# Removing the dummy matmuls that TensorE runs while it waits

## What is computed

```python
def _layernorm(x, g, b):
    mu = xf.mean(-1, keepdims=True)
    var = jnp.square(xf - mu).mean(-1, keepdims=True)
    return (xf - mu) * lax.rsqrt(var + LN_EPS) * g + b
...
    h_lat = _layernorm(ALPHA * h_lat + gt_m * mix, p['ln1_g'], p['ln1_b'])  # "ln1"
    moe = _hier_moe(_modulate(h_lat, sh_f, sc_f), p)  # routing 0, 32 experts
    h_lat = _layernorm(ALPHA * h_lat + gt_f * moe, p['ln2_g'], p['ln2_b'])  # "ln2"
...
        hn = rms_norm(h, attn_norm_g[l])  # "attn"
        proj = hn @ w_in[l]
...
        h = h + merged @ w_out[l]
        hn = rms_norm(h, ffn_norm_g[l])  # "ffn"
        h = h + hierarchical_moe(hn, ...)  # routing 1, 16 experts
    return rms_norm(h, final_norm_g)  # "final"
```

## Time and profile before

| | |
|---|---|
| median of 3 runs | 1681.69 us (1679.67 to 1684.29) |
| span of the profiled execution | 1681.9 us |
| TensorE busy | 1625.6 us, 97% of the span |
| DVE, ACT busy | 513.2 us, 295.8 us |
| granted TensorE clock, mean | 0.987 |

### The profile page before, as it was taken

The page is one execution under the profiler, slowest core; times in us unless marked ns, Lnnn a source line. Parts: engine busy times, 40 slices in busy tenths (PEclk is TensorE's granted clock), DMA queues, the critical chain, the costliest instruction groups (busy, mean ns, idle before and its releaser), DMA issues.

```text
span 1681.9 us, 22604 instructions
## 1 busy us (share of the span) xinstructions
PE 1625.6 (97%) x9324; PEld 1045.2 (62%) x9324; DVE 513.2 (31%) x1141; ACT 295.8 (18%) x470; POOL 16.7 (1%) x37
## 2 busy tenths in 40 slices
PE   5999999999999999999999999999999899999997
PEld 2877644664788885555555555557788775555554
DVE  1447685552001234222222222224023241222223
ACT  1100100221111012222122212222112022222222
POOL 0000000000000000000000000000100000000000
PEclk7999999999999999999999999999999999999999
DMA  9423231564333245999999999993632138999994
GB/s 393 178 100 113 100 113 56 214 243 161 131 126 144 101 164 196 396 416 414 406 412 414 408 413 403 411 388 127 187 143 100 51 150 338 413 403 417 409 410 180
DMA packets 33426, 434.88 MB, mean 259 GB/s; under 512 B 4048, under 2 KB 5592, under 8 KB 7144
## 3 DMA queue, kind: packets, MB, share of 16 engines
q1 hardware_dynamic: 29376, 423.64, 62.7%
q10 hardware_dynamic: 2328, 6.11, 1.5%
q0 software_dynamic: 1680, 4.52, 0.8%
HBM read 431.63 MB, written 2.62 MB: 258 GB/s over the span
## 4 chain that ended last, share of the span: by engine, by line
PE 91%; DVE 4%; DMA 1%; ACT 1%; issue 0%; ACTq 0%; DVEq 0%; SPq 0%
PE PP L629 24%; PE PP L878 20%; PE PP L635 12%; PE PP L905 10%; PE MB L855 6%; PE PP L841 5%; PE PP L847 2%; DMA ring<-in_w_moe 1%; PE MB L777 1%; PE PP L619 1%; PE PP L898 1%; PE MB L720 1%; PE MB L702 1%; PE MB L723 1%; PE MB L768 1%; PE PP L651 1%
## 5 line engine op out<-in xcount | busy, mean ns | idle before, releaser
L878 PE MATMUL PP<-ring,qd 128*64 128x256 f32 x3200 | 362.7, 379 | 2.2 <-ACT qd L541 1.8
L878 PEld LDWEIGHTS PP<-ring,qd 128*64 128x64 f32 x3200 | 228.8, 137 | 162.3 <-issue 35.0
L629 PE MATMUL PP<-uT,ring 128*128 128x256 f32 x1152 | 255.3, 384 | 3.7 <-ACT uT L389 2.7
L629 PEld LDWEIGHTS PP<-uT,ring 128*128 128x128 f32 x1152 | 221.7, 193 | 36.6 <-ACT uT L389 2.8
L905 PE MATMUL PP<-ring,qd 128*64 128x512 f32 x800 | 182.7, 599 | 0.0
L635 PE MATMUL PP<-ring,uT 128*128 128x512 f32 x288 | 125.0, 593 | 0.0
L1070 DVE SCALAR_TENSOR_TENSOR conv<-zpad,vec,conv 128x256 f32<-128x256 f32 x240 | 116.4, 485 | 8.6
L855 PE MATMUL MB<-V 64*128 64x256 f32 x832 | 117.5, 402 | 1.6 <-DVE V L1377 1.6
L905 PEld LDWEIGHTS PP<-ring,qd 128*64 128x64 f32 x800 | 52.9, 137 | 102.3 <-issue 102.3
L841 PE MATMUL PP<-Kc,V 128*64 128x512 f32 x416 | 98.2, 593 | 0.8 <-DVE V L1336 0.8
L635 PEld LDWEIGHTS PP<-ring,uT 128*128 128x128 f32 x288 | 54.5, 190 | 67.0 <-issue 66.9
(11 more groups left out here) (271 smaller groups left out, 1242.7 us busy)
## 6 DMA issues: line engine op xcount, KB each, us to landing
ring<-in_w_moe SPq DMA_DIRECT2D x150, 2048.0 KB, 10.6
ring<-in_w_ada SPq DMA_DIRECT2D x12, 2048.0 KB, 8.2
ring<-in_w_gates SPq DMA_DIRECT2D x8, 2048.0 KB, 7.8
ring<-in_w_v SPq DMA_DIRECT2D x5, 2048.0 KB, 7.7
ring<-in_w_glu SPq DMA_DIRECT2D x4, 2048.0 KB, 16.3
ring<-in_w_g SPq DMA_DIRECT2D x4, 2048.0 KB, 7.8
ring<-in_w_ret SPq DMA_DIRECT2D x4, 2048.0 KB, 7.6
ring<-in_w_q SPq DMA_DIRECT2D x3, 2048.0 KB, 9.6
```

The costliest lines, as they stand in the source:

```text
L629: ins = pe.matmul(out[:, c, :], W[:, k * width + at:k * width + at + P], X[:, k, :], start=k == 0, stop=k == K - 1)
L878: ins = pe.matmul(bank[q][SLOTS * g:SLOTS * (g + 1), 0:L], xts[:, k % 4, SLOTS * (k // 4):SLOTS * (k // 4 + 1)], ring[:, q, k * 512 + g * ...
```

## The change

All calls of keep_clock go, with the function, its constants and its table of PSUM regions. Nothing else changes: no wait, no order, no operand.

```diff
-MEAN_WAIT, SQUARE_WAIT, GAIN_WAIT, ATTN_WAIT = 7, 9, 24, 24
...
-            def keep_clock(n, spare):
-
-
-                for _ in range(n):
-                    pe.matmul(spare[:, 0:P], ident, ones, start=True, stop=True)
...
             def mean_sums(name, src):
 
-                if name != "conv":
-                    keep_clock(MEAN_WAIT, SPARE[name])
...
             def square_sums(name):
-                if name != "conv":
-                    keep_clock({"attn": ATTN_WAIT}.get(name, SQUARE_WAIT), SPARE[name])
...
                 cols = GROUPS + E
-                keep_clock(GAIN_WAIT, flat(MB[3]))
                 pe.wait_ge(ld_wr, 32)
...
                 turn_u(1)
 
-                keep_clock(14, flat(MB[0]))
                 pe.wait_ge(m["hot_ready"], 1)
...
                 pe.wait_ge(m["u_rows"], 1)
-                keep_clock(6, bank[3])
                 pe.wait_ge(m["g_ready"], 1)
...
             pe.wait_ge(b2["ld"], 16 * 12)
-            keep_clock(GAIN_WAIT - 4, bank[0])
```

More of the change, by code:

```diff
@@ L750, in _ @@
                 job(J["gates", b, 0])
-            def keep_clock(n, spare):
-                for _ in range(n):
-                    pe.matmul(spare[:, 0:P], ident, ones, start=True, stop=True)
-            SPARE = {"ln1": flat(MB[3]), "ffn": flat(MB[3]), "ln2": bank[0], "attn": bank[0], "final": bank[0]}
             def mean_sums(name, src):
-                if name != "conv":
-                    keep_clock(MEAN_WAIT, SPARE[name])
                 for k in range(DT):
```

## The result

The changed kernel takes 1692.84 us (median of 4; 1687.25 to 1694.37) against 1681.09 for the kernel before: ratio 1.0067, 95% interval 1.0046 to 1.0088; the medians are 11.8 us apart. A second series on another chip gave 1691.39 against 1680.11: ratio 1.0064 (1.0049 to 1.0079), 10.8 us slower (8.2 to 13.3); one of its 24 executions of the kernel before took 2141.53 us at a granted clock of 0.75 and is left out of the ratio. The forecast was 1697 with a range of 1688.5 to 1704.

What follows compares the result with a forecast made beforehand. TensorE, carrying 91% of the chain that ended last, was taken to bound the kernel. Half-clock losses of 17.6 us less 2.2 gained made +15.4 on 1681.7, forecast 1697 us, range 1688.5 to 1704.

Steps and rivals of the forecast that it cites:

- Rival B: All four places: only the long gaps bring the clock down, losses 12.4 us, time 1692; chance 0.17.
- late blocks: Dummies ahead of LayerNorm 1's mean and the ffn norm's squares hold up real work; removal gains 1.2 and 1.0 us.
- squares of ln1: LayerNorm 1: a bare 2.5 us gap ahead of the squares dips four times in five, costing 1.3 us.
- mean of ln2: Norm after the experts: 1.8 us idle after a short burst ahead of the mean, costing between 0 and 1.7, taken as 1.0.
- squares of ln2: Norm after the experts: a bare 2.5 us gap ahead of the squares, costing 1.3 us.
- final squares: Final norm: a short burst, then a bare 2.6 us gap ahead of the squares, costing 1.6 us.
- attention squares: Attention norm: 6.9 us idle ahead of the squares, certainly at half clock, costing 2.3 us.
- first job of block 2: Start of block 2: half clock after 6.2 us with only 0.8 us of work inside, costing 2.3 us.
- two routings: Both routings: half-clock logits +1.9, rank sums +1.1, rest of the gather 0.9; 3.9 us each, 7.8 together.
- Part 1: What dummies hold up now: only LayerNorm 1's mean and the ffn squares; removal frees 2.2 us in all.
- flat chance for a short gap: Bare gaps of about 2.5 us: four of five fall to half clock, so 0.8 x 1.6 = 1.3 us each.
- Rival C: Both routings stay at half clock until the expert loop, costing 6.9 us each, time 1703; chance 0.13.

Runs made afterwards that it cites:

- e1: The changed kernel (all dummies out) run again unaltered, as a second series on another chip against the kernel before: ratio 1.0064, 1691.39 us.
- e10: The changed kernel (all dummies out) run again unaltered for a third profile, one execution: 1691.99 us.
- e11: The changed kernel (all dummies out) run again unaltered for a fourth profile, one execution: 1687.00 us.

## Why the prediction came out as it did
It was right in sign and range and in its main mechanism, half clock behind bare gaps, and 4 us above the measured median. Rival B's number (1692) is closer than the forecast's, but its mechanism is refuted by the run with only the short gaps bare, and the number isn't that of its mechanism: its 7.8 us for the routings include what the forecast charged for the gap of 3.8 us ahead of the rank sums, which isn't over 5. Term by term, each cost being the length of the row less its length before, over four profiles of the changed kernel (after, e1, e10, e11):

| term | forecast | measured | mean |
|---|---|---|---|
| late blocks | -2.2 | -2.2 each time | -2.2 |
| squares of ln1 | 1.3 | 0, 0, 1.5, 0 | 0.4 |
| mean of ln2 | 1.0 | 0 each time | 0 |
| squares of ln2 | 1.3 | 0, 1.5, 1.5, 1.7 | 1.2 |
| final squares | 1.6 | 1.7 each time | 1.7 |
| attention squares | 2.3 | 2.6, 2.3, 2.3, 2.4 | 2.4 |
| first job of block 2 | 2.3 | 1.5, 3.0, 3.0, 1.4 | 2.2 |
| two routings | 7.8 | 4.8, 4.7, 4.7, 4.7 | 4.7 |
| sum | +15.4 | | +10.4 |

(The first job: half of the time that it ran at half clock.) The sum of the rows, 10.4, agrees with the 10.8 and 11.8 that the two series give.

- **Part 1** held to a tenth of a microsecond: the mean right behind the last mix job, the ffn squares in two bursts of 8 with 0.74 us between, 1.21 and 1.01 us gained.
- **The step that was off: what happens in the middle of the routing.** The forecast had another gap behind the turns, the rank sums cold behind it (+1.1), and 0.9 more for the gather. It took the gap from the kernel before, where TensorE reaches it at full clock. At half clock the logits end 1.7 us later and the turns (L798) take 3.62 us instead of 1.91; the work itself shortened the gap, from 3.85 us to 2.20, and the clock was back at 1.00 at 629.4, just when the turns had ended. The rank sums then ran at full rate (0.41 us a pair, as before). A new dip fell on the zero starts (4.52 us instead of 2.82), which lie beside DVE's chain. The gather took its 1.94. So the routing costs the logits' 1.7 and 0.6 more (0.8 in the second), not 3.9. Of those 0.6, 0.25 are the turned logits at half clock (L802, 0.69 us instead of 0.44), and some 0.2 come from a wait that the forecast had not seen: ACT copies the turned tokens before it makes DVE's exponentials, the slower turns delay that, and DVE waits for it (row of the changed kernel):

```profile
631.77 0.16 DVE L1283 TENSOR_REDUCE biasr<-biasr 128x2 f32<-128x8 f32 x1 [0.54 <-ACT biasr L534]
```

  The run with only the short gaps bare is the counterpart: there the clock is up when the turns start, the full 3.85 us are idle, and the rank sums do run at half rate, for 1.1 us in each routing (22.69 and 21.70 us to the loop instead of 21.60 and 20.51). The price of 1.1 was right, its condition was not. Nor is the shortened gap a rule: in the second routing of the kernel with only the routings bare, the logits ran at half clock too, and the rank sums went cold as forecast.
- **The flat chance for a short gap** was the second error: the mean of ln2 (1.88 us idle) never dipped, and the squares of ln1 did once in four. It was taken from five gaps of one execution. Together with the mean these are 1.9 us of the 5.0 that the forecast's sum has over the rows'; the routings are 3.1.
- **Rival C** (cold up to the loop) didn't happen: the clock came back at 629.4, and between the end of the logits at 623.98 and that moment TensorE ran nothing but the turns L802 and L798, 4.1 us of work. The rule behind it, that transposes don't raise the clock (TensorE: Matmul & The Clock Gate, PE-mode transpose, in the Trainium skill), isn't borne out by this, as far as the rows tell: they don't mark whether the turns ran in the mode that it speaks of, and the logits stood ahead of them.
- **The other rule weighed**, no idle gaps of more than about 3 us (TensorE: Matmul & The Clock Gate, Why this matters for your kernels, in the Trainium skill), is too mild here: gaps of 2.47 and 2.73 us cost 1.5 to 1.7 us in most executions.
- **A sign that failed:** the clock should have stood at 0.5 for some 20 to 30 us in the four places. It did for some 44 us in the first profile, because it also fell inside the waits and on the zero starts; the first job of block 2 held 14 to 20 records in its first 5.7 us, for 13 forecast and 27 before.
- The forecast took span and median as equal. A time is 1.8 us above its span, so the profiled execution of before was some 2 us slower than the median. Adding the difference to the median, as was done, was the right way round.

## What to carry over
Where engines take turns, a TensorE gap on the critical chain can cost twice: the wait, and the half-rate matmuls behind it; cheap full-width matmuls on constants, sized to end just before the operand comes, are worth their place (182 calls: 11 us here; four more blocks: 6 us). Price a dip by the row that it falls on and ask whether that row is on the chain; and work the gap out anew for the slower clock, since the longer work may fill part of it. A chance read from a few gaps of one execution is a guess: take several profiles of the same kernel before believing it.

## What the runs showed of the hardware
- How often an idle gap of TensorE was followed by half clock, over the 14 profiles of this study (only gaps behind the first 50 us that TensorE entered at full clock; counted is a fall between the gap's start and 3.5 us behind its end):

| idle gap, place | bare in | half clock behind it |
|---|---|---|
| 1.41 to 1.88 us, several places | 28 | 0 |
| 1.94 to 2.00, rank sums of routing 1 | 5 | 4 |
| 2.09, ahead of the second attention turn | 14 | 6 |
| 2.20, ahead of the pb jobs | 12 | 0 |
| 2.46, squares of ln1 | 5 | 1 |
| 2.47, squares of ln2 | 5 | 4 |
| 2.65, ahead of the out2 jobs | 12 | 12 |
| 2.71, ahead of the first scores | 12 | 7 |
| 2.73, final squares | 5 | 4 |
| 3.08, ahead of the mix jobs | 12 | 12 |
| 2.76 and 3.13, logits, with 12 dummies ahead | 2 | 0 |
| 2.29 to 3.85, rank sums | 5 | 5 |
| 3.19 to 6.9, logits, attention squares, first job of block 2 | 26 | 26 |

  In these profiles none of the gaps up to 1.88 us was followed by half clock and every one from 3.19 us up was; between them the place decided more than the length: 2.20 us never, 2.65 always. Executions run much alike up to a few us, so these are not independent draws; why one place is safe and its neighbour is not was not settled.
- Weight loads with 2 streamed columns did not hold the clock (0.50 behind the dummies, where it was 1.00 with 128 columns), though the profile counts TensorE as busy.
- From execution to execution the changed kernel varies by 7 us (1687 to 1694); the profiles show a good part of it in the dips of block 2 (185.6 to 188.9 us), without any change of the code there.
